# Shared keys and values of the second block: compression in its projection's wake, its tail among the next feed-forward's first matmuls

## What is computed

```python
def nsa_shared_kv(s, kv_norm, kv_w, cmp_pe, cmp_w1, cmp_w2, k_norm):
    kv = rmsnorm(s, kv_norm) @ kv_w
    kc, vc, ks, vs, kw, vw = [a.reshape(B, T, N_KVH, HEAD_DIM) for a in jnp.split(kv, 6, axis=-1)]
    idx = jnp.arange(n_cmp)[:, None] * CMP_STRIDE + jnp.arange(CMP_BLOCK)[None, :]

    def compress(a, pe, w1, w2):
        blk = a[:, idx] + pe[:, None, :]
        flat = blk.transpose(0, 1, 3, 2, 4).reshape(B, n_cmp, N_KVH, CMP_BLOCK * HEAD_DIM)
        return jax.nn.silu(flat @ w1) @ w2

    k_cmp = rmsnorm(compress(kc, cmp_pe[0], cmp_w1[0], cmp_w2[0]), k_norm[0])
    v_cmp = compress(vc, cmp_pe[1], cmp_w1[1], cmp_w2[1])
    ks = rmsnorm(ks, k_norm[1])
    kw = rmsnorm(kw, k_norm[2])
    return (k_cmp, v_cmp, ks, vs, kw, vw)
```

## Time and profile before

| | us |
|---|---|
| median of 3 executions (2108.79 to 2113.75) | 2109.05 |
| the profiled execution's own time | 2109.34 |
| its span in the profile | 2107.1 |
| PE busy | 2011.1 (95%) |
| DVE busy | 1209.4 (57%) |
| ACT busy | 1009.6 (48%) |

### The profile page before, as it was taken

The page is one execution under the profiler, slowest core; times in us unless marked ns, Lnnn a source line. Parts: engine busy times, 40 slices in busy tenths (PEclk is TensorE's granted clock), DMA queues, the critical chain, the costliest instruction groups (busy, mean ns, idle before and its releaser), DMA issues.

```text
span 2107.1 us, 26160 instructions
## 1 busy us (share of the span) xinstructions
PE 2011.1 (95%) x9910; PEld 1682.3 (80%) x9910; DVE 1209.4 (57%) x1808; ACT 1009.6 (48%) x1561; POOL 59.2 (3%) x70
## 2 busy tenths in 40 slices
PE   7999989999999799998999997999968999899999
PEld 5888978888888698887888886888867888788887
DVE  5555646556555657555655645655646555676554
ACT  5444555445443665444544435544545444455442
POOL 1000300000000000000000000000000000200000
PEclk9999999999999799999999999999989999899999
DMA  9555425555555315553555333655435553305550
GB/s 314 192 193 167 147 94 200 179 180 180 181 191 179 110 41 192 193 192 132 200 179 185 134 121 127 208 191 192 140 111 189 179 188 132 100 1 196 191 191 21
DMA packets 239914, 338.92 MB, mean 161 GB/s; under 512 B 5496, under 2 KB 205343, under 8 KB 239695
## 3 DMA queue, kind: packets, MB, share of 16 engines
q1 hardware_dynamic: 239134, 336.15, 47.4%
q0 software_dynamic: 496, 1.23, 0.2%
q10 hardware_dynamic: 192, 0.30, 0.0%
HBM read 336.61 MB, written 1.05 MB: 160 GB/s over the span
## 4 chain that ended last, share of the span: by engine, by line
PE 92%; DVE 4%; ACT 2%; POOL 1%; issue 1%; DMA 0%; SPq 0%; ACTq 0%; DVEq 0%; POOLq 0%
PE A L490 10%; PE A L491 10%; PE A L492 10%; PE G L490 10%; PE G L491 10%; PE G L492 10%; PE X L490 8%; PE X L492 8%; PE X L491 8%; PE A L1016 2%; DVE wl L486 1%; PE G L805 1%; PE A L763 1%; PE X L805 1%; PE X L1003 1%
## 5 line engine op out<-in xcount | busy, mean ns | idle before, releaser
L486 DVE TENSOR_TENSOR wl<-raw,wh 128x1024 fp32r<-128x1024 f32 x557 | 658.3, 1223 | 178.5 <-ACT wh L477 178.1
L477 ACT ACTIVATE wh<-raw 128x1024 fp32r<-128x1024 f32 x557 | 564.7, 1057 | 178.4 <-PE A L492 128.3
L490 PE MATMUL G<-wh,xh 128*128 128x512 f32 (+1 forms) x816 | 325.4, 399 | 14.4 <-DVE xl L1946 14.4
L491 PE MATMUL G<-wl,xh 128*128 128x512 f32 (+1 forms) x816 | 319.8, 392 | 0.0
L492 PE MATMUL G<-wh,xl 128*128 128x512 f32 (+1 forms) x816 | 319.8, 392 | 0.0
L490 PE MATMUL X<-wh,xh 128*128 128x512 f32 x672 | 265.6, 395 | 0.0
L492 PE MATMUL X<-wh,xl 128*128 128x512 f32 x672 | 262.0, 390 | 0.0
L491 PE MATMUL X<-wl,xh 128*128 128x512 f32 x672 | 261.7, 389 | 0.0
L490 PEld LDWEIGHTS G<-wh,xh 128*128 128x128 f32 x816 | 154.7, 190 | 46.5 <-issue 15.3
L492 PEld LDWEIGHTS G<-wh,xl 128*128 128x128 f32 x816 | 154.7, 190 | 33.0
L491 PEld LDWEIGHTS G<-wl,xh 128*128 128x128 f32 x816 | 155.0, 190 | 30.3
(11 more groups left out here) (421 smaller groups left out, 2770.3 us busy)
## 6 DMA issues: line engine op xcount, KB each, us to landing
raw<-in_ffn_w_in SPq DMA_DIRECT2D x88, 1024.0 KB, 6.7
raw<-in_ffn_w_gate SPq DMA_DIRECT2D x44, 1024.0 KB, 5.5
raw<-in_ffn_w_up SPq DMA_DIRECT2D x44, 1024.0 KB, 7.5
raw<-in_ffn_w_down SPq DMA_DIRECT2D x44, 1024.0 KB, 6.2
raw<-in_ffn_w_out SPq DMA_DIRECT2D x44, 1024.0 KB, 7.0
raw<-in_a_w_in SPq DMA_DIRECT2D x12, 1024.0 KB, 6.1
raw<-in_ab_w_in SPq DMA_DIRECT2D x8, 1024.0 KB, 7.1
raw<-in_kv_w SPq DMA_DIRECT2D x6, 1024.0 KB, 6.3
```

What stands on the lines that cost most here:

```text
L477: nc.scalar.activation(hi, r, ACT.Copy).then_inc(hi_done[u], 1)
L486: nc.vector.tensor_tensor(lo, r, hi.bitcast(F32), ALU.subtract).then_inc(lo_done[u], 1)
L490: nc.tensor.matmul(o, sh, rh, start=start, stop=False)
L491: nc.tensor.matmul(o, sh, rl, start=False, stop=False)
```

## The change

All that is moved lies between the projection of the phase kv and `step(1)` of ffn6. The number of instructions on PE stays the same.

- PE makes the transposes of the compression inputs two half-tiles earlier (`i == 6`). The 96 matmuls of the compression follow the projection: the first kind at once, then `turn_stream("ffn6", 0)`, then the second kind. They accumulate in X0 and X1, and the small products use other columns of the same two banks. Only then come the key transposes, now into G0, G1, A1, A3.
- The tail is cut in three: the first kind's small transposes and products stay in `kv_stage`; the second kind's small transposes (`compress_turn(1)`) stand behind `turn_stream("ffn6", 1)` in the middle of `gate_up(0, 0)`; the 64 small products and the key transpose (`compress_last`) stand between `gate_up(0, 0)` and `gate_up(0, 1)`. The wait for `kv_done` stands before `step(1)`, and two waits for `kv_k_out` guard the banks G and A.
- ACT and DVE make `cT` and both `blk` during the projection, prepare the compression's weights during it too, and DVE sums the key squares in two parts of 8 groups. Both then run a new `with_compress` in place of the usual entry to ffn6, in which the tiles and chunks of ffn6 stand between the steps of the tail.
- `hkr` and `hk` move to other columns of `work`, so that `ksw` is not overwritten.

The diff, cut to its core:

```diff
-                   hkr=cut(work, 1024, 2, CMP_HID), hk=cut(work, 1536, 2, 2, 60), kcn=cut(work, 2100, P),
+                   hkr=cut(work, 0, 2, CMP_HID), hk=cut(work, 512, 2, 2, 60), kcn=cut(work, 2100, P),
...
-        KV_C, KV_K = (A[2], A[3], G[0], G[1]), (X[0], X[1], A[0], A[1])
+        KV_C, KV_K = (A[2], A[3], G[0], G[1]), (G[0], G[1], A[1], A[3])
@@ -753,8 +753,6 @@
...
-                    if name == "ffn6" and half == 0:
-                        pe.wait_ge(event("kv_done"), 5)
                     pe.wait_ge(h_ready, HALF_READY[name][half])
@@ -786,7 +784,11 @@
...
                             if half == 0 and i == 2:
+                                if name == "ffn6":
+                                    pe.wait_ge(event("kv_k_out"), 4)
                                 turn_stream(name, 1)
+                                if name == "ffn6":
+                                    compress_turn(1)
                             wait_chunk(name, 4 * half + i)
@@ -835,10 +837,16 @@
...
-                if BEFORE.get(name) is None or joined(BEFORE[name]) is None:
+                if name != "ffn6" and (BEFORE.get(name) is None or joined(BEFORE[name]) is None):
                     turn_stream(name, 0)
+                if name == "ffn6":
+                    pe.wait_ge(event("kv_k_out"), 2)
                 gate_up(0, 0)
+                if name == "ffn6":
+                    compress_last()
                 gate_up(0, 1)
+                if name == "ffn6":
+                    pe.wait_ge(event("kv_done"), 5)
                 step(1)
@@ -1240,7 +1248,7 @@
...
                 for i, e in enumerate(ROWS["kv"]):
-                    if i == 8:
+                    if i == 6:
                         pe.wait_ge(event("kv_c_out"), 2)
@@ -1250,7 +1258,26 @@
...
+                def compress(kind, part):
+
+                    pe.wait_ge(event("kv_blk_lo"), kind + 1)
...
+                            last = mm3(X[kind][0:60, 0:CMP_HID], bh[:, j0 + j, :], bl[:, j0 + j, :], sh[:, j, :],
...
+
+                pe.wait_ge(row_out, ROW_OUT["kv"] - 1)
+                compress(0, [(4, 0, 0), (5, 0, 4), (4, 1, 8), (5, 1, 12)])
                 pe.wait_ge(row_out, ROW_OUT["kv"])
+                pe.wait_ge(event("kv_c_cols"), 4)
+                turn_stream("ffn6", 0)
+                compress(1, [(4, 2, 0), (5, 2, 4), (6, 0, 8), (7, 0, 12)])
+                compress_turn(0)
                 pe.wait_ge(event("kv_dup"), 2)
...
-                pe.wait_ge(event("kv_k_out"), 4)
-                pe.wait_ge(event("kv_c_cols"), 4)
...
-                for kind in range(2):
-                    pe.wait_ge(event("kv_act"), kind + 1)
...
                 pe.wait_ge(event("kv_hk"), 1)
...
-                    last = mm(A[2][0:60, 0:HD], nsa["hk"][:, 0, c, :], w2[:, 0, c, :], start=c == 0, stop=c == 1)
...
+
+            def compress_turn(kind):
+
+                pe.wait_ge(event("kv_act"), kind + 1)
...
+                last.then_inc(event("kv_h_turned"), 1)
+
+            def compress_last():
+
@@ -1785,10 +1812,40 @@
...
+                block_hi(0)
+                selected_out(0)
+                prep("kv", 4, (0,))
+                block_hi(1)
                 prep("kv", 5, (0,))
+                prep("kv", 4, (1,))
+                prep("kv", 5, (1,))
+                prep("kv", 4, (2,))
                 selected_out(1)
-                prep("kv", 4, (1, 2))
-                prep("kv", 5, (1, 2))
+
+            def with_compress():
+
...
+                prep("kv", 5, (2,))
+                prep("kv", 6)
+                prep("kv", 7)
+                prep("ffn6", 0, (1,))
+                gate(0)
+                for i in range(4):
+                    chunk_hi("ffn6", i)
+                prep("ffn6", 1, (1,))
+                prep("ffn6", 0, (0,))
+                gate(1)
+                hidden_out(0)
                 for b, bank in enumerate(KV_K):
                     act.wait_ge(event("kv_k_turned"), b + 1)
                     dst = (nsa["kS"], nsa["kW"])[b // 2][:, 2 * (b % 2):2 * (b % 2) + 2, :]
@@ -1796,35 +1853,28 @@
                         act.wait_ge(event("kv_gain"), 1)
                     A_(dst, bank[:, :].rearrange("p (g s) -> p g s", g=2), ACT.Copy,
                        scale=k_gain[:, 1 + b // 2:2 + b // 2]).then_inc(event("kv_k_out"), 1)
-                for kind in range(2):
...
-                prep("kv", 6)
...
-                    act.wait_ge(event("kv_h_turned"), kind + 1)
...
+                prep("ffn6", 1, (0,))
+                for i in range(4, 6):
+                    chunk_hi("ffn6", i)
+                squares("ffn6")
+                for i in range(6, KC):
+                    chunk_hi("ffn6", i)
+                hidden_out(1)
+                prep("ffn6", 0, (2,))
                 act.wait_ge(event("kv_v2"), 1)
                 act.wait_ge(event("kv_zero"), 2)
                 for r in range(4):
 
                     at = slice(CP * r, CP * r + NCMP)
@@ -2400,29 +2443,74 @@
...
+                blocks(0)
+                blocks_lo(0)
+                blocks(1)
+                key_sums(0)
+                prep("kv", 4, (0,))
+                blocks_lo(1)
                 V.memset(nsa["vC"], 0.0).then_inc(event("kv_zero"), 1)
-                for kind in range(2):
+                prep("kv", 5, (0,))
+                prep("kv", 4, (1,))
+                prep("kv", 5, (1,))
+                prep("kv", 4, (2,))
+                key_sums(1)
+                V.tensor_scalar(nsa["ms"][:, 0:16], nsa["ss"][:, 0:16], 1.0 / HD, EPS, ALU.mult, ALU.add
+                                ).then_inc(mx_ready, 1)
+
+            def with_compress():
+
...
+                prep("kv", 5, (2,))
+                prep("kv", 6)
+                dve.wait_ge(mx_pow, 2)
...
+                    V.tensor_tensor(dup[:, :, d, :], k, wide(nsa["rs"][:, 0:16].unsqueeze(2), 16, HD), ALU.mult
+                                    ).then_inc(event("kv_dup"), 1)
+                prep("kv", 7)
+                gate(0)
+                prep("ffn6", 0, (1,))
+                for i in range(4):
+                    chunk_lo("ffn6", i)
+                prep("ffn6", 1, (1,))
+                prep("ffn6", 0, (0,))
+                gate(1)
...
+                prep("ffn6", 1, (0,))
+                for i in range(4, 6):
+                    chunk_lo("ffn6", i)
...
                 last.then_inc(event("kv_kcn"), 1)
-                prep("kv", 8, (0, 1))
-                prep("kv", 9, (0, 1))
+                for i in range(6, KC):
+                    chunk_lo("ffn6", i)
+                means(NORM["ffn6"])
```

More of the change, by code:

```diff
@@ L1295, in kv_stage @@
                 pe.wait_ge(event("kv_kcn"), 1)
-                nc.tensor.transpose(X[0][:, 0:60], nsa["kcn"][0:60, :], ident[0:60, 0:60]).then_inc(event("kv_kc"), 1)
+                nc.tensor.transpose(X[0][:, 448:508], nsa["kcn"][0:60, :], ident[0:60, 0:60]).then_inc(event("kv_kc"), 1)
             def nsa_mixer():
@@ L1777, in selected_out, with block_hi @@
                     last.then_inc(row_out, 1)
-                selected_out(0)
-                prep("kv", 4, (0,))
+                def block_hi(kind):
+                    act.wait_ge(event("kv_blk"), kind + 1)
+                    A_(mhf[:, 960 * kind:960 * (kind + 1)], nsa["blk"].rearrange("p j r -> p (j r)"), ACT.Copy
+                       ).then_inc(event("kv_blk_hi"), 1)
                 for b in range(4):
@@ L1956, in norm_stream, with means @@
                     chunk_lo(name, i)
+                means(n)
+                for i in range(4, KC):
+                    chunk_lo(name, i)
+            def means(n):
                 for t in range(NT):
@@ L1960, in norm_stream @@
                                     ).then_inc(ms_ready, 1)
-                for i in range(4, KC):
-                    chunk_lo(name, i)
             def small_weights():
@@ L2006, in ffn @@
                     prep(name, 1, (0, 1))
-                norm_stream(name)
+                if name == "ffn6":
+                    with_compress()
+                else:
+                    norm_stream(name)
                 prep(name, 0, (2,))
@@ L2406, in kv_stage, with key_sums @@
                     dve.wait_ge(event("kv_blk_lo"), kind + 1)
-                prep("kv", 6)
-                V.memset(nsa["vC"], 0.0).then_inc(event("kv_zero"), 1)
-                for kind in range(2):
+                def key_sums(br):
+                    part = slice(4 * br, 4 * br + 4)
+                    dve.wait_ge(event("kv_ksw"), 2 * br + 2)
+                    link(V.tensor_tensor(sq[:, :, part, :], keys[:, :, part, :], keys[:, :, part, :], ALU.mult))
+                    link(V.tensor_reduce(ss[:, :, part], sq[:, :, part, :], AX.X, ALU.add))
```

107 lines of the change are left out of this document (46 added, 61 removed).

## The result

The changed kernel takes 2085.03 us (median of 4 executions, 2084.44 to 2085.24), beside 2108.94 us (4 executions, 2108.79 to 2113.75) for the kernel before: ratio 0.9881, 95% interval 0.9864 to 0.9898. That is 23.9 less, where 22.5 were forecast; 2085.0 was the time of rival 1, in which the clock holds. The profiled execution took 2085.24 with a span of 2083.4, 23.7 shorter than before.

The account below looks back on a forecast made before the run. PE, busy 95%, bounds the kernel, so gain comes from its gaps or low clock. `step(1)` starting 24.1 earlier, less 1.6 for a clock fall, gives 22.5: median 2086.5 us, range 2083 to 2091.

Parts of the forecast that it names:

- rival 1: PE's clock holds through the waits before ffn6, no low stretch: 24.1 gained, 2085.0 us; chance 0.28.
- The gap and the cover: After the projection, the first compression kind's 5.6 of PE work runs without a wait, covering 3.7 of the key chain.
- the 9.49 and the 5.33: PE's idle times in the kernel before, ahead of the key transposes and ahead of the compression; both forecast gone.
- POOL's power: Power in the key chain, beside two DVE low parts: taken as 3.8, bounds 2.9 and 5.2; DVE idle beside it before, 2.91.
- Rival 3: POOL's power is held by both DVE low parts, 5.2 instead of 3.8: 2087.9 us; chance 0.09.
- The four waits: PE idles before the key product 1.9, ffn6's first matmul 0.8, the 64 value products 0.7 and `step(1)` 0.9.
- The walk: Step-by-step timing of PE, ACT and DVE queues in their new order, from projection to `step(1)`, which begins 24.1 earlier.
- The clock: Waits before the key product and ffn6, 2.7 idle within 3.1, make PE's clock fall for about 3, costing 1.6.
- The loads: ffn6 weights land 5.6 after issue; the up tile, wanted by ACT at 47.5, lands at 49.1, delaying only the sigmoid.
- rival 2: A late ffn6 weight, deciding from a landing about 8 after issue: 18.5 gained, 2090.5 us; chance 0.13.
- Nothing is given back: From `step(1)` on, queues hold the same instructions in the same order, so the gain stays whole.
- rival 5: ffn6 never catches up: PE waits for low parts in 10 further steps, slower, 2116.5 us at 3 a step; chance 0.03.

Follow-up runs that it names:

- e3_idle_beside_power: Changed kernel with DVE's low parts of two compression tiles moved from beside POOL's power to behind the key products; 2090.02 us, ratio to the kernel before 0.9894.
- e5_order_of_act: Changed kernel with the same instructions in another order on ACT and DVE; 2082.21 us, beside 2084.74 for the changed kernel run again as control.
- e4_gap_a: Changed kernel with one useless 128x1024 copy added on ACT ahead of `hidden_out(0)`; 2090.79 us, ratio to the kernel before 0.9895.
- e1_tail_before_ffn6: Changed kernel with the whole tail and the wait for `kv_done` put back ahead of ffn6's first matmul; 2093.62 us, ratio to the kernel before 0.9918.
- e4_gap_b: Changed kernel with three useless 128x1024 copies added on ACT ahead of `hidden_out(0)`; 2090.64 us, ratio to the kernel before 0.9897.

## Why the prediction was right, and where it was off

**The gap and the cover.** Right. The first kind starts at 1543.22, 0.23 behind the last projection matmul, and takes 5.62 to the stream's transposes at 1548.84; the 9.49 and the 5.33 are gone without a gap of their own.

**POOL's power.** Right. 3.8 was taken, between 2.9 and 5.2, by the one row with a DVE neighbour; 3.81 was measured, and `e3_idle_beside_power` shows that the neighbour is the cause. Rival 3 did not happen. Low part of the last compression tile: forecast through at 53.6, measured 1553.62 (DVE's gate stands there). DVE's walk held to 0.3 up to this point.

**The four waits.** Forecast 1.9, 0.8, 0.7 and 0.9, measured 1.31, 0.65, 0.30 and 0.89. The first was 0.6 too long, the third 0.4. The walk has a slip at the third: 64.2 + 0.9 + 2.1 + 0.9 + 0.3 is 68.4 and not 68.0, so by its own terms that wait was 1.1, which is 0.8 too long, and every later time, the forecast's too, was 0.4 higher. ACT was ahead of my walk: through with `hidden_out(0)` at 1558.57 + 0.25 = 1558.8 (timeline of ACT) instead of 59.3, while PE came 0.3 later. The sum was 1.15 too high. Against it stood PE's own work, 0.4 too low in the walk: `gate_up(0, 0)` took 7.13 (1560.02 to 1567.45 - 0.30) instead of 6.8, the rest lies in the transposes. `e5_order_of_act` gives PE's work by itself, without a wait and at the upper clock: 30.84 from the start of the last projection matmul, 30.6 from its end, where the sum had 30.1. So two errors of opposite sign, and the walk's 34.8 from the end of the projection stood against 34.1.

**The clock.** The step that failed. I had two rows of similar gaps, one followed by a fall and one not the earlier trace rows, and took the fall, at 1.6. In the changed kernel the clock was 1.00 over the whole stretch: the gap was 1.31 + 0.65 = 1.96 and not the 2.7 of the walk, and no fall came. `e4_gap_a` shows that the question was the right one and the margin thin: with 0.95 more of waiting the fall was there, in the execution that was profiled. The price can't be called right or wrong: the two falls of `e1_tail_before_ffn6` cost 2.7 together by J less the waits (6.0 - 3.3), 1.6 and 1.5 by the matmuls behind them, so each was near the forecast, while those of `e4_gap_a` and `e4_gap_b` cost 2.9 and 2.2, since the low stretch there was near 7 (about 1560.7 to 1567.6 in `e4_gap_b`) and not 3. Had the fall come, the time would have been, as an estimate, 2085.0 and 1.4 to 2.9 more: 2086.4 to 2087.9.

**The loads.** The up tile was to land at 49.1, 5.6 after its issue. The timeline of ACT shows when it did:

```profile
1551.18 1.06 ACT L477 ACTIVATE wh<-raw 128x1024 fp32r<-128x1024 f32 x1 [3.35 <-DMA raw<-in_ffn_w_in]
```

That is 2.1 later, some 7.6 after its issue and so close to the 8 of rival 2, and it cost nothing: DVE came to the sigmoid's product at 1553.62, as forecast. ACT stood for 3.35 there, and was still ahead of my walk when PE asked for it.

**Nothing is given back.** Nearly right. ffn6 has no gap behind `step(1)`, so rival 5 is out. But 0.7 was lost in nsa to a low clock that came sooner there, which I had excluded on the ground that "the queues hold the same instructions in the same order".

**The sum.** Forecast 24.1 - 1.6 = 22.5. Measured on the profiled executions: 24.83 in J, less 0.25 by a later start, less about 0.9 given back, 23.7. Rival 1, the same walk without the fall, has the time to a tenth; that it is so near is in part luck, since it rests on two small errors of opposite sign, on the slip of 0.4 and on the 0.9 that was given back. The forecast itself lies within 1.5 of the result although the one event that it chose, the fall, did not happen, because the price that it put on it was small.

## What to carry to other kernels

Where PE waits for a chain through three engines, look for matmuls that need nothing of it and put them into the chain's time, and place the chain's last pieces between large matmuls of the next phase rather than ahead of it: here that was worth 24.8 of 59.2, 19.1 of it waiting and 5.7 the low clock behind the waits. Then walk the helpers' queues once more: their order alone held another 3.5. Add to each wait that is left the low clock it may bring, since here, in the one profiled execution, a wait 1 us longer cost almost 4.
